# Preparing the first up-projection step's weights inside the last group of the out-projection, and a new order for VectorE's turns

## The reference

```python
mix = jnp.einsum('bte,ed->btd', mix, w_out)
x = layer_norm(DEEPNORM_ALPHA * x + mix, ln1_g, ln1_b)

up = jnp.einsum('btd,df->btf', x, w_up)        # 1024 x 5632
hp = jnp.concatenate([conv_prefix, up], axis=1)
hc = conv_b + sum(conv_w[i] * hp[:, i:i + T] for i in range(CONV_WIDTH))
g, u = hc[..., :D_FF], hc[..., D_FF:]
y = jnp.einsum('btf,fd->btd', jax.nn.gelu(g, approximate=False) * u, w_down)
x = layer_norm(DEEPNORM_ALPHA * x + y, ln2_g, ln2_b)
```

## Time and profile before

| | us |
|---|---|
| median of three runs (2396.57 to 2401.55) | 2398.47 |
| the profiled execution, own time | 2398.07 |
| its span, first to last instruction | 2396.3 |
| PE busy (share of the span) | 2244.6 (94%) |
| DVE busy | 1655.8 (69%) |
| ACT busy | 980.8 (41%) |
| POOL busy | 782.8 (33%) |
| layer 0: last group of the out-projection on PE | about 380.0 to 417.5 |
| layer 0: the seven products of step 0 | 419.5 to 467.5 |
| layer 1: the same two stages | about 1563 to 1600.5, 1602.6 to 1650.8 |

### The profile page before, as it was taken

The page is one execution under the profiler, slowest core; times in us unless marked ns, Lnnn a source line. Parts: engine busy times, 40 slices in busy tenths (PEclk is TensorE's granted clock), DMA queues, the critical chain, the costliest instruction groups (busy, mean ns, idle before and its releaser), DMA issues.

```text
span 2396.3 us, 35859 instructions
## 1 busy us (share of the span) xinstructions
PE 2244.6 (94%) x14276; PEld 2025.5 (85%) x14276; DVE 1655.8 (69%) x2014; ACT 980.8 (41%) x1773; POOL 782.8 (33%) x444
## 2 busy tenths in 40 slices
PE   7999899799999999999999998987999999999996
PEld 7997677699999998887799876767999999987875
DVE  1558747777777776777636586486777777767777
ACT  2227634543443444333412375454344344443332
POOL 1115234434434440220311342344443444402202
PEclk9999989899999999999999999998999999999999
DMA  5412145122222224755551213541222222255762
GB/s 149 99 29 64 57 152 164 45 83 66 73 83 71 68 83 151 276 201 183 188 132 45 56 38 102 144 152 45 65 74 83 69 70 83 83 222 197 249 213 95
DMA packets 207974, 269.50 MB, mean 112 GB/s; under 512 B 31952, under 2 KB 166584, under 8 KB 207736
## 3 DMA queue, kind: packets, MB, share of 16 engines
q1 hardware_dynamic: 207808, 267.21, 36.5%
HBM read 217.39 MB, written 46.13 MB: 110 GB/s over the span
## 4 chain that ended last, share of the span: by engine, by line
PE 56%; DVE 20%; ACT 7%; issue 5%; DMA 4%; POOL 4%; SPq 2%; DVEq 0%; ACTq 0%; POOLq 0%
PE ps L2056 23%; PE ps L1770 13%; PE ps L1735 9%; PE ps L1995 3%; DMA wblk<-in_w_up 3%; DVE rl L1424 2%; POOL bl L733 2%; SPq L528 2%; DVE bnst L1252 1%; DMA wrow<-in_w_down 1%; POOL wblk L741 1%; PE ps L1795 1%; ACT bh L938 1%; PE ps L1874 1%; DVE bl L1356 1%
## 5 line engine op out<-in xcount | busy, mean ns | idle before, releaser
L2056 PE MATMUL ps<-bt,bh 128*128 128x272 f32 x3520 | 598.2, 292 | 29.9 <-issue 19.7
L2056 PEld LDWEIGHTS ps<-bt,bh 128*128 128x128 f32 x3520 | 503.5, 191 | 37.3 <-issue 25.9
L938 ACT ACTIVATE bh<-wblk 128x512 fp32r<-128x512 f32 x308 | 183.6, 624 | 542.8 <-POOL wblk L745 237.5
L2056 PE MATMUL ps<-bt,bl 128*128 128x272 f32 x1760 | 367.3, 290 | 0.0
L1356 DVE TENSOR_TENSOR bl<-wblk,bh 128x512 fp32r<-128x512 f32 x210 | 165.2, 803 | 182.2 <-ACT bh L938 182.2
L2056 PEld LDWEIGHTS ps<-bt,bl 128*128 128x128 f32 x1760 | 278.7, 191 | 0.0
L733 POOL TENSOR_TENSOR bl<-wblk,bh 128x512 fp32r<-128x512 f32 x98 | 163.3, 1669 | 310.8 <-ACT bh L938 310.8
L1770 PE MATMUL ps<-rh,ah 128*128 128x512 f32 x792 | 246.3, 392 | 14.7 <-DVE rzd L1238 6.5
L2056 PE MATMUL ps<-ba,bh 128*128 128x272 f32 x1408 | 238.4, 292 | 9.0 <-POOL bl L733 4.1
L1770 PE MATMUL ps<-rl,ah 128*128 128x512 f32 x792 | 244.1, 389 | 0.0
L1424 DVE TENSOR_TENSOR rl<-wrow,rh 128x1024 fp32r<-128x1024 f32 x132 | 191.6, 1452 | 51.0 <-ACT rh L994 51.0
(11 more groups left out here) (223 smaller groups left out, 4081.4 us busy)
## 6 DMA issues: line engine op xcount, KB each, us to landing
wrow<-in_w_down SPq DMA_DIRECT2D x132, 512.0 KB, 4.7
wblk<-in_w_up SPq DMA_DIRECT2D x88, 512.0 KB, 5.2
a_scr<-hg SPq DMA_DIRECT2D x44, 552.0 KB, 3.4
araw<-a_scr SPq DMA_DIRECT2D x88, 192.0 KB, 4.5
wrow<-in_w_out SPq DMA_DIRECT2D x48, 256.0 KB, 5.5
wrow<-in_w_out SPq DMA_DIRECT2D x24, 512.0 KB, 4.0
wraw<-in_w_in SPq DMA_DIRECT2D x10, 1024.0 KB, 6.0
z_scr<-rzc SPq DMA_DIRECT2D x16, 512.0 KB, 3.7
```

Source lines behind the costliest of these rows:

```text
L938: act.activation(bh[b][:], block_of(f, b), ACT.Copy).then_inc(S["u_hi"], 1)
L2056: e = nc.tensor.matmul(out[:, n, :], lhs, rhs[:, HW_ // 2 * n:HW_ // 2 * n + HW_ // 2], start=(k == 0 and m == 0), stop=(k == HK - 1 and m ...
```

## The change

SP loads the weights of step 0 earlier, in the second group of the out-projection, once that group's products are done; they go to a free piece of `btf` (columns of tile 7) and not to `wblk`. The high parts of B_11 and B_12 are made by ACT behind `hi_out(22)` and `hi_out(23)`, and go with their low parts to columns of tile 6 in the same array. POOL makes the low part of B_11 behind `lo_out(20)`, that of B_12 behind `lo_out(21)`, the sums S1 and S2 behind `lo_out(22)` and the other two behind `lo_out(23)`. The sums are written to `wblk`, no longer in place. Since tokens' operands will take the same columns, DVE waits for product B_12 ahead of tile 6's sums, and for POOL's sums and its low part of B_22 ahead of tile 7's. The high parts of B_S2, B_S1, B_22 and B_S3 stand between the layer norm's and the operands' instructions on ACT; step 1's high parts wait for other products than before, since B_22 and B_S3 of step 0 use other buffers. On DVE the last group's order becomes: turned of the next tile, then the low part of this tile, then the next tile's sums.

```diff
@@ -369,7 +369,23 @@

             s0 = (2 + 2 * f) % 4
             which, k0 = {B_11: (0, 0), B_12: (0, HK), B_S2: (0, 0), B_S1: (1, 0), B_22: (1, HK), B_S3: (1, HK), B_S4: (0, HK)}[b]
+            if f == 0 and b in (B_11, B_12, B_22):
+                return quarter(which, k0)
             return wblk[s0 + which][:, k0:k0 + HK, :]
+
+        def quarter(which, k0):
+
+            return btf[:, 32 - 8 * which + k0:36 - 8 * which + k0, first_cols(NB - 1)]
+
+        def split_of(f, b):
+
+            if f:
+                return bh[b], bl[b]
+            if b < B_S2:
+                r, cols = 32 - 8 * b, first_cols(NB - 2)
+                return bt[:, r:r + HK, cols], bt[:, r + HK:r + 8, cols]
+            i = {B_S2: 0, B_S1: 1, B_S3: 2, B_22: 3, B_S4: 6}[b]
+            return bh[i], bl[i]

         def half(f, which, h):

@@ -442,14 +458,15 @@
             def up_cols(l, f):
                 s0 = (2 + 2 * f) % 4
                 if f == 0:
-                    sp.wait_ge(S["w_lo"], l * WIO + INT + OUTU - 2)
+                    sp.wait_ge(S["c_done"], l * NTOK + 6)
                 elif f == 1:
                     sp.wait_ge(S["w_lo"], l * WIO + INT + OUTU)
                 else:
                     sp.wait_ge(S["u_lov" if f > 2 else "u_lop"], lo_n(l, f - 2, B_S4))
                 for which in range(2):
                     c = DFF * which + P * f
-                    sp.dma_start(wblk[s0 + which][:], w_up[l, :, c:c + P].rearrange("(k p) n -> p k n", p=P))\
+                    dst = wblk[s0 + which][:] if f else btf[:, 32 - 8 * which:40 - 8 * which, first_cols(NB - 1)]
+                    sp.dma_start(dst, w_up[l, :, c:c + P].rearrange("(k p) n -> p k n", p=P))\
                         .then_inc(S[f"wu_landed{f % 2}"], 16)

             def down_row(l, d):
@@ -640,8 +657,10 @@
                         c = KD * (g + 1) + kk
                         if c < OUTU:
                             out_row(l, c)
-                        elif c < OUTU + 2:
-                            up_cols(l, c - OUTU)
+                        elif c == OUTU:
+                            up_cols(l, 1)
+                        if c == OUTU - 3:
+                            up_cols(l, 0)

                         if 5 <= kk < 8:
                             z_rows(l, C3[g][kk - 5])
@@ -730,7 +749,25 @@

             def lo_up(l, f, b):
                 pool.wait_ge(S["u_hi"], 7 * (l * FT + f) + SPLIT.index(b) + 1)
-                pool.tensor_tensor(bl[b][:], block_of(f, b), bh[b][:].bitcast(F32), ALU.subtract).then_inc(S["u_lop"], 1)
+                high, low = split_of(f, b)
+                pool.tensor_tensor(low[:], block_of(f, b), high[:].bitcast(F32), ALU.subtract).then_inc(S["u_lop"], 1)
+
+            def sum_first(l, b):
+
+                n = 4 * l * FT
+                a11, a12, a21, a22 = (quarter(*q) for q in ((0, 0), (0, HK), (1, 0), (1, HK)))
+                s1, s2, s3, s4 = (block_of(0, q) for q in (B_S1, B_S2, B_S3, B_S4))
+                if b == B_S1:
+                    pool.wait_ge(S["wu_landed0"], 32 * (l * (FT // 2) + 1))
+                    pool.tensor_tensor(s1, a21, a22, ALU.add).then_inc(S["u_sum"], 1)
+                elif b == B_S2:
+                    pool.wait_ge(S["u_sum"], n + 1)
+                    pool.tensor_tensor(s2, s1, a11, ALU.subtract).then_inc(S["u_sum"], 1)
+                elif b == B_S4:
+                    pool.wait_ge(S["u_sum"], n + 2)
+                    pool.tensor_tensor(s4, a12, s2, ALU.subtract).then_inc(S["u_sum"], 1)
+                else:
+                    pool.tensor_tensor(s3, a22, s2, ALU.subtract).then_inc(S["u_sum"], 1)

             def sum_up(l, f, b):

@@ -748,7 +785,7 @@
                     pool.wait_ge(S["u_sum"], n + 2)
                     pool.tensor_tensor(a12, a12, a11, ALU.subtract).then_inc(S["u_sum"], 1)
                 else:
-                    pool.wait_ge(S["u_lov" if f else "u_lop"], lo_n(l, f, B_22))
+                    pool.wait_ge(S["u_lov"], lo_n(l, f, B_22))
                     pool.tensor_tensor(a22, a22, a11, ALU.subtract).then_inc(S["u_sum"], 1)

             def residual(l, t):
@@ -788,15 +825,16 @@
                 rotate(l, NB - 1)
                 for c in range(1, OUTU):
                     lo_out(l, c)
-                lo_up(l, 0, B_11)
-                lo_up(l, 0, B_12)
-                for b in (B_S1, B_S2, B_S4):
-                    sum_up(l, 0, b)
-                for b in (B_S2, B_S1, B_22):
+
+                    if OUTU - 4 <= c < OUTU - 2:
+                        lo_up(l, 0, (B_11, B_12)[c - OUTU + 4])
+                    elif c == OUTU - 2:
+                        sum_first(l, B_S1)
+                        sum_first(l, B_S2)
+                sum_first(l, B_S4)
+                sum_first(l, B_S3)
+                for b in SPLIT[2:]:
                     lo_up(l, 0, b)
-                sum_up(l, 0, B_S3)
-                lo_up(l, 0, B_S3)
-                lo_up(l, 0, B_S4)
                 for f in range(1, FT):
                     lo_up(l, f, B_11)
                     lo_up(l, f, B_12)
@@ -921,13 +959,16 @@
                     act.wait_ge(S[f"wu_landed{f % 2}"], 32 * (l * (FT // 2) + f // 2 + 1))
                 elif b in SUMS:
                     act.wait_ge(S["u_sum"], 4 * n + SUMS.index(b) + 1)
-                if f:
+                if f > 1 or f == 1 and b == B_S4:

                     act.wait_ge(S["u_p"], 7 * (n - 1) + b + 1)
-                elif b < 4:
-                    name, count = used_c(l, OUTU - 2 + b // 2)
+                elif f == 1 and b < B_S3:
+
+                    act.wait_ge(S["u_p"], 7 * (n - 1) + {B_11: B_S2, B_12: B_S1, B_S2: B_S3, B_S1: B_22}[b] + 1)
+                elif f == 0 and b in (B_S2, B_S1, B_S3, B_22):
+                    name, count = used_c(l, OUTU - 2 + (b in (B_S3, B_22)))
                     act.wait_ge(S[name], count)
-                else:
+                elif f == 1 or b == B_S4:

                     act.wait_ge(S["z_tr"], (l + 1) * NTOK)
                     for q in range(3):
@@ -935,7 +976,7 @@
                     if b == B_S4:

                         act.wait_ge(S["u_u2"], l * FT + 1)
-                act.activation(bh[b][:], block_of(f, b), ACT.Copy).then_inc(S["u_hi"], 1)
+                act.activation(split_of(f, b)[0][:], block_of(f, b), ACT.Copy).then_inc(S["u_hi"], 1)

             def snap(l, f):

@@ -1135,6 +1176,8 @@
                         c = KD * g + kk
                         if c + 2 < OUTU:
                             hi_out(l, c + 2)
+                        if g == 2 and kk in (4, 5):
+                            block_hi(l, 0, (B_11, B_12)[kk - 4])
                         if g == 0 and kk == 7:
                             act.wait_ge(S["s_pe"], 6 * l + 6)
                             act.activation(hT[:, T_Q:T_Q + 4, SEQ:T], ps[:, 6, 0:4 * NS].rearrange("p (j q) -> p j q", q=NS), ACT.Copy)\
@@ -1142,19 +1185,19 @@
                             m_hi(l, 5)
                 t0, t1, t2 = C3[2]
                 deviation(l, 0, t0)
-                block_hi(l, 0, B_11)
                 normal(l, t0)
-                block_hi(l, 0, B_12)
                 deviation(l, 0, t1)
                 normal(l, t1)
+                block_hi(l, 0, B_S2)
                 deviation(l, 0, t2)
                 normal(l, t2)
+                block_hi(l, 0, B_S1)
                 turned(l, t0)
                 operand_hi(l, t0, 0)
-                block_hi(l, 0, B_S2)
+                block_hi(l, 0, B_22)
                 turned(l, t1)
                 operand_hi(l, t1, 0)
-                block_hi(l, 0, B_S1)
+                block_hi(l, 0, B_S3)
                 turned(l, t2)
                 operand_hi(l, t2, 0)
                 for part in (1, 2):
@@ -1162,8 +1205,6 @@
                         operand_hi(l, t, part)
                     if part == 1:
                         snap(l, 0)
-                        block_hi(l, 0, B_22)
-                block_hi(l, 0, B_S3)


                 for f in range(FT):
@@ -1302,6 +1343,12 @@
                     b12, b22 = mix[:, 0:HK, right], mix[:, HK:KD, right]
                     t1, t2, t3, t4 = (btf[:, 24 + 4 * i:28 + 4 * i, cols] for i in range(4))
                     n = ts_n(l, t, 4 * side)
+                    if t == NB - 2:
+
+                        dve.wait_ge(S["u_p"], 7 * l * FT + B_12 + 1)
+                    elif t == NB - 1:
+                        dve.wait_ge(S["u_lop"], lo_n(l, 0, B_22))
+                        dve.wait_ge(S["u_sum"], 4 * l * FT + 4)
                     if side == 0:
                         dve.wait_ge(S["xf_ev"], c_n(l, t) + 1)
                         dve.wait_ge(S["xf_dv"], c_n(l, t) + 1)
@@ -1342,10 +1389,8 @@
                 elif t < NB:
                     operand_sums(l, t)
                     dve.wait_ge(S["t_sum"], ts_n(l, t, 2))
-                    operand_lo(l, t, 0)
-                    if t not in C3[2]:
-                        operand_lo(l, t, 1)
```

(23 more changed lines are left out.)

## The result

The changed kernel takes 2408.12 us (median of 20 runs, 2403.01 to 2411.97). In the same sessions the kernel before took 2398.93 (20 runs, 2394.15 to 2404.62). The ratio is 1.0041, with a 95% interval of 1.0035 to 1.0048: by this ratio slower by 9.8 us (8.4 to 11.5). The prediction said 2405, 2397 to 2410, with 0.62 on slower.

A forecast was written before the change was run, and what follows sets the result against it. The prediction took DVE, with ACT in its cadence, to bound the stretch around the out-projection's end, not the weights. Per layer 6.2 - 1.1 - 1.9, rounded, gave +3.3 us, twice +6.6: median 2405, range 2397 to 2410.

The forecast's parts named there:

- sign: Whole kernel: slower, median from 2398.47 to 2405 us; chance 0.62 on slower.
- main mechanism: End of each layer's out-projection: POOL's added work makes row 23's low part 7.2 us late, stalling PE and delaying DVE.
- The three low parts on POOL: Out-projection's last group: low parts of rows 21, 22, 23 done at 407.6, 413.2, 418.3; PE stalls 0.6, about 2, 4.6 us.
- The layer norm's start: DVE, last group: the layer norm starts 4.7 us later, at 419.05, because PE's first tile is late.
- The bound on POOL's new work: Beside DVE's tile 8: four new POOL instructions take 1.3 us each, or 1.6 disturbed; up to 1.3 more per layer.
- The clock behind the stops: PE's second tile, last group: the clock falls after the stops, adding 1.5 us to DVE's chain.
- ACT's block against the small scale instruction: Before the first tile's turned: ACT's B_S1 block adds up to 0.6 us, DVE's scale instruction loses about as much.
- The new order: DVE, last group: the next tile's turned hides in the pause, saving 1.1 us over two changes of tile.
- Part 2: DVE's three low parts of part 2: 2.1 us instead of 4.04, with POOL's work moved ahead; 1.9 us won.
- B_S4: Product B_S4: starts 10.0 us after B_S3 before and after, so the +3.3 us delay passes through to the end.
- number 3: Rival, slower still: DVE's lock stretches POOL's new work, part 2 stays slow; +5 to +6 us per layer, 2409 to 2410; chance 0.15.
- number 2: Rival, faster: row 23's low part is late by less than the slack; each layer wins 3.2 us, median 2392; chance 0.15.

The follow-up runs named there:

- x1: The changed kernel with all of POOL's new work for step 0 moved behind row 23's low part; 1.0027 of the kernel before.
- x4: The kernel before with only DVE's new order for the last group; 1.0000 of the kernel before.
- x6: x5 with POOL's low parts of B_22 and B_S3 held until DVE's third sums, their high parts made earlier on ACT; 0.9965 of the kernel before.
- x5: x1 with POOL waiting to start the new work until DVE has joined the group's first tile; 0.9994 of the kernel before.
- x8: x7 with 16 extra matmuls, never read, behind B_S1 in step 0 so PE doesn't stand still ahead of B_S3; 0.9962 of the kernel before.
- x7: The kernel before with DVE making v, u3 and c22 of step 0 ahead of step 1's low part of B_S2; 0.9971 of the kernel before.
- x2: The changed kernel with only the sums S1 and S2 moved on POOL behind row 23's low part; 1.0022 of the kernel before.

## Why the prediction was right, and where its sum was off

The sign and the main mechanism were right, and 2408.1 lies in the range. The forecast of +3.3 us per layer is measured as +5.7 and +5.4. Step by step, on the clock of before:

- **The three low parts on POOL.** Row 21's ends at 407.5 (predicted 407.6), row 22's at 412.9 (413.2), row 23's at 418.7 (418.3). PE's stops of 0.50, 1.88 and 5.10 are those foretold (0.6, about 2, 4.6).
- **The layer norm's start, +4.7 predicted, +5.7 measured** (422.72 - 2.62 = 420.10, against 414.37). The bound on POOL's new work named stretched POOL instructions, and the sums did take 1.45 and 1.59. The clock, too, was already low on row 23's own low part: its two products take 1.22, not 0.73. And by x1 tile 8 would be late by 5.5 with no stall at all. The forecast gave the collision a direction, POOL losing to DVE; it is DVE that loses where POOL works without gaps. In the changed kernel itself tile 8 ends at 418.86 on the clock of before, 4.4 late, so the forecast's 4.7 would nearly have come about without its mechanism.
- **The clock behind the stops, +1.5 predicted, +1.1 measured.** DVE joins the second tile 3.78 us after the first (422.72 to 426.50), before 2.70. The prediction's ground for it, that each stop of some two microseconds or more costs about 1.7, is too wide: ahead of B_11 the kernel before has a stop of 2.04 us, and its products keep to full clock, 0.73 us for the first four and 0.66 for later ones.
- **ACT's block against the small scale instruction, set against each other.** ACT's block costs 0.5 (the pause of 1.42 is 1.94); from the second tile's joining to the first `turned` DVE takes 7.38 instead of 8.07, with two of its three scale instructions at 0.16, so 0.7 is won. Near enough. DVE's chain is late by 5.7 + 1.1 - 0.7 + 0.5 = 6.6 at the first tile's sums, predicted 6.2.
- **The new order, -1.1 predicted, +0.3 measured: the step that failed.** "With the next tile's `turned` inside the pause, it is hidden" is true, but it brings the low part onto POOL's B_22 and B_S3, each 2.19 instead of 1.23. The forecast had weighed that collision for part 2 and not for the tiles themselves. x4 shows it alone, x6 its absence.
- **Part 2, -1.9 predicted, -2.15 measured**: 1.89 us against the 4.04 of the earlier trace rows. B_S3 starts at 457.10 on the clock of before, 4.2 late, predicted 456.
- **B_S4, +3.3 predicted, +4.7 measured** (467.57, against 462.87). By the terms, 6.6 + 0.3 - 2.15 = 4.75. "B_S4 starts 10.0 us after B_S3 does" came out as 10.5, because the chain starts with u2 and not with B_S3: in the kernel before B_S3 waited for POOL's low part until u2 was made, now it starts as soon as c11 is there, 0.5 us ahead of u2. From u2 to B_S4 it is 10.0 and 9.9.
- **Not priced: the clock at B_S4, +1.0.** PE stood idle 4.23 us ahead of it, against 2.27 before, and its granted clock from there to step 1 is 0.76 instead of 0.84; the stretch takes 11.63 instead of 10.65. That the longer stop is the cause is likely and not shown (see x6). 4.7 + 1.0 is the 5.7 of the layer.

So two terms make up the 2.4 us that the layer lost beyond the forecast: the new order (1.4) and the clock at B_S4 (1.0); the others, off by +1.0, -0.4, -0.2 and -0.25, nearly cancel, which is luck. Of the rivals, number 3 gave the time (2409 to 2410) with half of its mechanism: the collision was there, but in the low parts of the tiles, while part 2 became fast. Number 2 counted 2.5 us of slack on DVE for tile 8; by x1 that slack isn't there, since tile 8 slips under the same POOL work.

The collision has a page. The Trainium skill, SBUF — State Buffer, in "SBUF: two separate sides", describes an exclusive lock between GpSimd and a VectorE instruction with two SBUF inputs; the traces agree (2.19 against 1.23 in x4 and x6), and also in that `turned`, which reads PSUM, keeps its 1.36 beside POOL in x6.

## What to carry to other kernels

Before work is put into an idle place of one engine, look up what the other engines do at that very time: here POOL was free, but a row that PE wanted next stood behind it in the queue, and DVE's last instructions ahead of the critical tile stood beside it. Work that nobody needs yet can be held back with a wait on the event after which it harms no one (x5), and placed beside instructions that it doesn't disturb (x6). A gain of one place must be followed to the next bound, since x8's 1.4 us were gone one step later, and nearly half of x7's three steps later.

## What the runs showed of the hardware

- When POOL works back to back it is DVE that loses most: instructions of 0.69 us take 1.76 and 1.78, one of 0.29 takes 1.35 (x1), while POOL's own 1.29 grows to 1.34 to 1.71. The layer norm came 5.5 us late by this alone.
- A stop of PE of 2.62 us is followed by products at the lower of the two clock levels (four products 1.25 us instead of 0.74), one of 0.68 isn't (x7, x8). Behind 4.23 us four products take 1.24 and then three times 1.11 us, until 475.77, in the changed kernel. The length of the stop alone doesn't decide when the clock falls: behind 3.40 us in x2 the first four products take 0.74 and the next three fours 0.90, 1.11 and 1.11; behind 2.27 in layer 0 of the kernel before they take 1.17, behind 2.46 in its layer 1 0.73.
